# Attention heads in a hand-scheduled decoder trunk: probabilities divided before the transpose, values as the stationary operand, two heads on two column halves, layers written out

## The reference, cut to what matters

```python
# branch A: sparse keys (top-k of an indexer), branch C: causal, branch D: window of 128, with a sink
dots = jnp.einsum('bthd,bsd->bths', qib, ki32)                       # indexer of branch A
iscore = jnp.einsum('bth,bths->bts', wib, jax.nn.relu(dots))
...
s = jnp.where(mask, q @ k.T * scale - slope * dist, NEG)
p = jax.nn.softmax(s, axis=-1)                                       # D: the sink is one more column
o = jnp.einsum('bhts,bshd->bthd', p, v).reshape(B, BLOCK, -1)
...
proj = jnp.einsum('bsnw,nwd->bsnd', ys, w_branch)                    # ys: the four branches' outputs
return jnp.sum(sigmoid(gates) * proj, axis=2) @ w_out
```

## Time and profile before

| | |
|---|---|
| median of 3 runs (lowest, highest) | 2903.86 us (2902.56, 2909.98) |
| profiled execution: its own time | 2905.41 us |
| its span, first to last instruction | 2903.5 us |
| mean granted TensorE clock | 0.992 |
| TensorE matmul / weight load busy | 96% / 79% |
| VectorE / ScalarE / GpSimd busy | 55% / 36% / 6% |
| data moved | 329 MB, 113 GB/s |

### The profile page before, as it was taken

How to read it: one execution, slowest core, us unless ns; L and a number is a source line. 1 busy time by engine, 2 the same in 40 slices (tenths; PEclk the granted TensorE clock), 3 DMA queues, 4 the chain that set the end, 5 groups by cost and what they waited for, 6 DMA issues and landing times.

```text
span 2903.5 us, 40034 instructions
## 1 busy us (share of the span) xinstructions
PE 2793.0 (96%) x13408; PEld 2285.5 (79%) x13408; DVE 1608.6 (55%) x2682; ACT 1038.1 (36%) x1859; POOL 165.5 (6%) x175
## 2 busy tenths in 40 slices
PE   4999999999999999999989999999999999999998
PEld 4888887677778788888878888877777778888887
DVE  6655445667555646633266663466675456565323
ACT  2322234444444433222232222344444453432223
POOL 0111000000000001110011110000000000011100
PEclk9999999999999999999999999999999999999999
DMA  5655422111212224532235544221112223164232
GB/s 229 231 188 181 145 90 77 48 52 59 73 51 95 87 80 174 197 99 94 95 117 202 188 161 143 90 66 52 52 64 68 67 79 102 51 224 174 94 101 95
DMA packets 89157, 329.26 MB, mean 113 GB/s; under 512 B 10018, under 2 KB 10402, under 8 KB 87587
## 3 DMA queue, kind: packets, MB, share of 16 engines
q1 hardware_dynamic: 88994, 327.25, 32.9%
HBM read 325.11 MB, written 2.10 MB: 113 GB/s over the span
## 4 chain that ended last, share of the span: by engine, by line
issue 58%; PE 34%; DVE 2%; DMA 2%; POOL 1%; ACT 1%; DVEq 1%; SPq 0%; ACTq 0%; POOLq 0%
PE bank L447 11%; PE bank L448 11%; PE bank L449 11%; DMA ada_raw<-ada 1%; DMA ada_start<-ada 1%; DVE x L1256 1%; DVEq L1286 1%; PE bank L1455 1%; ACT squares_out L817 1%; POOL wi L571 0%; POOL row_sum L561 0%; POOL rstd_diag L563 0%; DVE ada_start L1327 0%; DVE w_low L431 0%; PE bank L1513 0%
## 5 line engine op out<-in xcount | busy, mean ns | idle before, releaser
L447 PE MATMUL bank<-h_high,w_high 128*128 128x512 f32 (+1 forms) x2528 | 979.1, 387 | 31.1 <-DVE h_low L1277 17.3
L449 PE MATMUL bank<-h_high,w_low 128*128 128x512 f32 (+1 forms) x2528 | 960.7, 380 | 0.0
L448 PE MATMUL bank<-h_low,w_high 128*128 128x512 f32 (+1 forms) x2528 | 960.0, 380 | 0.0
L431 DVE TENSOR_TENSOR w_low<-w_raw,w_high 128x1024 fp32r<-128x1024 f32 x440 | 569.5, 1295 | 606.0 <-ACT w_high L425 603.7
L425 ACT ACTIVATE w_high<-w_raw 128x1024 fp32r<-128x1024 f32 x440 | 461.3, 1050 | 361.7 <-PE bank L456 331.9
L447 PEld LDWEIGHTS bank<-h_high,w_high 128*128 128x128 f32 x2528 | 481.9, 191 | 125.6 <-issue 19.4
L449 PEld LDWEIGHTS bank<-h_high,w_low 128*128 128x128 f32 x2528 | 480.8, 190 | 90.5
L448 PEld LDWEIGHTS bank<-h_low,w_high 128*128 128x128 f32 x2528 | 481.6, 191 | 86.3 <-issue 2.4
L454 PE MATMUL bank<-w_high,ffn_high 128*128 128x512 f32 x704 | 275.6, 391 | 0.0
L456 PE MATMUL bank<-w_low,ffn_high 128*128 128x512 f32 x704 | 273.9, 389 | 0.0
L455 PE MATMUL bank<-w_high,ffn_low 128*128 128x512 f32 x704 | 273.9, 389 | 0.0
(11 more groups left out here) (197 smaller groups left out, 2664.9 us busy)
## 6 DMA issues: line engine op xcount, KB each, us to landing
w_raw<-stream SPq DMA_DIRECT2D x444, 512.0 KB, 3.5
ada_raw<-ada SPq DMA_DIRECT2D x144, 512.0 KB, 3.6
ada_start<-ada SPq DMA_DIRECT2D x8, 1024.0 KB, 16.4
mixer_consts<-mixc SPq DMA_DIRECT2D x2, 1152.0 KB, 5.2
x<-x_in SPq DMA_DIRECT2D x1, 2048.0 KB, 18.1
silu_c<-silu_row SPq DMA_DIRECT2D x4, 512.0 KB, 4.5
out<-x SPq DMA_DIRECT2D x8, 256.0 KB, 2.0
lru_w<-lruw SPq DMA_DIRECT2D x2, 512.0 KB, 3.6
```

What stands on the lines that cost most here:

```text
L431: eng.tensor_tensor(wL[:, slot], raw[:, slot], wH[:, slot].bitcast(F32), ALU.subtract).then_inc(lo_ready[slot].sem, 1)
L447: eng.matmul(o, a, rhs_h, start=first, stop=False)
L448: eng.matmul(o, a, rhs_l, start=False, stop=False)
L449: return eng.matmul(o, b, rhs_h, start=False, stop=last)
```

## The change

What it does:

- Attention: POOL computes the reciprocal of each head's row sum (192 powers with exponent -1), ScalarE multiplies the probabilities by it in place, one step after the exp, and the transposes take the divided probabilities. The lag of the transposes is 3 steps and that of the values 4 (2 and 3 before). There are 4 score slots and 3 slots of transposed probabilities (3 and 2 before).
- The values (64 columns) are the stationary operand and the transposed probabilities (128 columns) the moving one. In every odd step the two heads of a pair are multiplied, alternating over the key blocks, head e into partitions 64e to 64e+63 of bank 7. The result is feature-major, so `y_tok`, its division and its four transposes per block are gone; `y_high` and `y_low` are made from bank 7. The rows of `w_branch` for A and D are permuted on the host to match. A branch has 37 steps.
- D's sink is one more column of the scores (a copy of one column on VectorE for each head), so the sink's own sum and exp are gone.
- Indexer: the dots of a pair of heads are issued together in every even entry, into four banks (4 to 7); entry n waits for the relu of entry n-3.
- The loops over the layers are written out. In the second layer two of three chunks of the modulation product are left out in the second FFN, and so are the loads and splits of the weights of a third layer, and, in the last `closing`, the squares and means of x and their powers.

The core of the diff:

```diff
-TR_LAG, PV_LAG = 2, 3
-END_LAG = HEADS - 1 + PV_LAG
-YT_LAG = END_LAG + 1
+TR_LAG, PV_LAG = 3, 4
+Y_LAG = HEADS - 1 + PV_LAG + 1
...
+def ada_chunks(l, f):
+    return ADA_FFN[f] - (2 if f == 1 and l == DEPTH - 1 else 0)
+
+def ends(l, n):
+    return l == DEPTH - 1 and n == 2
...
+            def reciprocals(l, br, st):
+                g = att_index(br, st)
+                b, h, _, _ = keys(br, st)
+                c = 8 * (b % 2) + h
+                pool.wait_ge(probs_ready.sem, probs_ready.at(l, g + 1))
+                pool.tensor_tensor(recip[:, g % 8:g % 8 + 1], rsum[:, c:c + 1], mone, ALU.pow
+                                   ).then_inc(recip_ready.sem, 1)
...
-            with pool.Fori(0, DEPTH) as l:
+            for l in range(DEPTH):
...
+                    if 1 <= st < STEPS + 1:
+                        g = att_index(br, st - 1)
+                        b, h, k0, nk = keys(br, st - 1)
+                        s.wait_ge(recip_ready.sem, recip_ready.at(l, g + 1))
+                        s.activation(s_sb[:, g % S_SLOTS, 0:P * nk], s_sb[:, g % S_SLOTS, 0:P * nk], ACT.Copy,
+                                     scale=recip[:, g % 8:g % 8 + 1]).then_inc(norm_ready.sem, 1)
...
                     b, h = it[1], it[2]
                     n = HEADS * (b - 1) + h
-                    if n >= 2:
-                        pe.wait_ge(relu_ready.sem, relu_ready.at(l, n - 1))
...
-                    rows = slice(64 * (h % 2), 64 * (h % 2) + 64)
-                    pe.matmul(bank[4 + n % 2][:, 0:P * (b + 1)], iq[rows, h // 2, b * P:(b + 1) * P],
-                              ik[rows, 0:P * (b + 1)], start=True, stop=True).then_inc(dots_ready.sem, 1)
+                    if n >= 4 and n % 2 == 0:
+                        pe.wait_ge(relu_ready.sem, relu_ready.at(l, n - 2))
+                    for i in range(2 if n % 2 == 0 else 0):
+                        rows = slice(64 * i, 64 * i + 64)
+                        pe.matmul(bank[4 + (n + i) % 4][:, 0:P * (b + 1)], iq[rows, h // 2, b * P:(b + 1) * P],
+                                  ik[rows, 0:P * (b + 1)], start=True, stop=True).then_inc(dots_ready.sem, 1)
...
-            if PV_LAG <= st < STEPS + PV_LAG:
+            if PV_LAG <= st < STEPS + PV_LAG and (st - PV_LAG) % 2:
                 g = att_index(br, st - PV_LAG)
+                pair = (st - PV_LAG) % HEADS // 2
                 pe.wait_ge(pt_evicted.sem, pt_evicted.at(l, g + 1))
-                if h == 0 and g > 0:
-                    pe.wait_ge(ytok_ready.sem, ytok_ready.at(l, g // HEADS))
-                for i in range(nk):
...
-                    mm = pe.matmul(bank[7][:, h * HD:(h + 1) * HD], pt_sb[:, g % 2, i * P:(i + 1) * P], vv,
-                                   start=i == 0, stop=i == nk - 1)
+                if pair == 0 and g > 1:
+                    pe.wait_ge(ylo_ready.sem, ylo_ready.at(l, g // HEADS))
+                for i in range(keys(br, st - PV_LAG)[3]):
+                    for e in range(2):
+                        b, h, k0, nk = keys(br, st - PV_LAG - 1 + e)
...
+                        mm = pe.matmul(bank[7][HD * e:HD * e + HD, pair * P:(pair + 1) * P], vv,
+                                       pt_sb[(g - 1 + e) % PT_SLOTS][:, i * P:(i + 1) * P], start=i == 0,
+                                       stop=i == nk - 1)
                 mm.then_inc(pv_done.sem, 1)
-            blk = (st - YT_LAG) // HEADS
-            if st >= YT_LAG and (st - YT_LAG) % HEADS == 0:
...
-                for t in range(4):
-                    mm = pe.transpose(bank[2 + use % 2][:, t * P:(t + 1) * P], y_tok[:, t * P:(t + 1) * P],
-                                      ident[:, :])
-                mm.then_inc(ytr_ready.sem, 1)
```

More of the change, by code:

```diff
@@ L236, in trunk_kernel @@
         S0 = M0 + 57 * K
[L237 to L238 removed]
+        s_sb = at("scores_sb", [P, S_SLOTS, T], F32, S0)
+        pt_sb = [at(f"probs_t{i}", [P, T], F32, w) for i, w in enumerate((S0 + 8 * K, S0 + 10 * K, X0 + 8 * K))]
         relu_sb = at("relu_dots", [P, 2, T], F32, S0 + 6 * K)
[L240 removed]
         bias_sb = at("bias_sb", [P, T], F32, X0 + 10 * K)
@@ L547, in _, with att_index, keys @@
             sp.wait_ge(stored.sem, 16 * 2 * TB)
-            for slot in range(RING):
-                sp.wait_ge(raw_full[slot].sem, raw_full[slot].at(DEPTH, 16))
+        def att_index(br, st):
+            return STEPS * ATT.index(br) + st
+        def keys(br, st):
+            b, h = st // HEADS, HEAD_AT[br][st % HEADS]
+            k0 = max(0, b - 1) if br == "D" else 0
+            return b, h, k0, b + 1 - k0
         @block.gpsimd
@@ L592, in _ @@
                                            ).then_inc(rs_ready.sem, 1)
+                        for br in ATT:
+                            for st in range(STEPS):
+                                reciprocals(l, br, st)
                         closing(l, 1)
@@ L734, in scalar_mixer @@
                     br, st = it[1], it[2]
+                    blk = (st - Y_LAG) // HEADS
+                    if st >= Y_LAG and (st - Y_LAG) % HEADS == 0:
+                        s.wait_ge(pv_done.sem, pv_done.at(l, (att_index(br, 0) + HEADS * (blk + 1)) // 2))
+                        s.activation(yH[Y_OF[br]][:, :, blk * P:(blk + 1) * P],
+                                     bank[7][:, :].rearrange("p (t n) -> p t n", t=4), ACT.Copy
+                                     ).then_inc(yhi_ready.sem, 1)
                     if TR_LAG <= st < STEPS + TR_LAG:
@@ L861, in _ @@
                 squares_x(i // 2, i % 2)
-            with s.Fori(0, DEPTH) as l:
+            for l in range(DEPTH):
                 opening(l, -1, U_FFN[0])
@@ L1156, in vector_attention @@
                 first = nsink[:, h:h + 1] if br == "D" else 3e38
-                v.tensor_tensor_reduce(s_sb[:, g % 3, 0:w], bank[4 + g % 2][:, 0:w], bias, 1.0, first, ALU.add,
+                if br == "D":
+                    v.tensor_copy(s_sb[:, g % S_SLOTS, w:w + 1], nsink[:, h:h + 1])
+                v.tensor_tensor_reduce(s_sb[:, g % S_SLOTS, 0:w], bank[4 + g % 2][:, 0:w], bias, 1.0, first, ALU.add,
                                        ALU.min, nmax[:, c:c + 1]).then_inc(shifted.sem, 1)
-            if br == "C":
-                token_y(v, l, br, st)
-            blk = (st - YT_LAG) // HEADS
-            if st >= YT_LAG and (st - YT_LAG) % HEADS == 0:
+            blk = (st - Y_LAG) // HEADS
+            if st >= Y_LAG and (st - Y_LAG) % HEADS == 0:
                 g = TB * ATT.index(br) + blk
@@ L1211, in vectors @@
                                        ALU.mult, ALU.mult)
-                pre_vector(which)
+                if not ends(l, which):
+                    pre_vector(which)
             def gain_build(l, n):
@@ L1280, in opening @@
                     j = i % KD
-                    if i == 2 and n >= 0:
+                    if i == 2 and (n >= 0 or l > 0):
                         mean_x(l, n, TB - 1)
@@ L1330, in _ @@
             v.scalar_tensor_tensor(vecA[:, :], mod[:, 8 * KD:9 * KD], 1.0, parv[:, 2 * KD:3 * KD], ALU.add, ALU.mult)
-            with v.Fori(0, DEPTH) as l:
+            for l in range(DEPTH):
                 v.drain()
@@ L1691, in _ @@
             pe.wait_ge(consts_in.sem, 16 * 5)
-            with pe.Fori(0, DEPTH) as l:
+            for l in range(DEPTH):
                 for f in range(2):
@@ L1776, in _mixer_units @@
             w = w_branch[branch_at[it[1]]]
+            if it[1] in "AD":
+                w = w[np.concatenate([pairs(0, j) for j in range(4)])]
             out.append(np.concatenate([_tile(w, P * (2 * it[2] + m) + r(P)) for m in range(2)], axis=2))
```

168 lines of the change are left out of this document (62 added, 106 removed).

## The result

The changed kernel takes **2861.47 us** (median of 4, 2861.17 to 2864.06); the kernel before, beside it, 2906.92 (4 runs, 2902.56 to 2910.71). The ratio is 0.9846, 95% interval 0.9828 to 0.9864: 45 us less by the medians, and 44 between the two profiled runs, for which 29 were forecast.

What follows compares the result with a forecast made beforehand. The prediction took TensorE, with a matmul in flight for 96% of the span, as the bound. Its terms summed to -28.8 us from 2905.4, giving 2876.6, less 1.6 to the median: 2875 us; own range 2858 to 2890, whole range 2848 to 2900.

Steps and rivals of the forecast that it cites:

- The indexer: Indexer of both layers: dots in pairs and four banks let TensorE leave 3 to 6.5 us earlier per layer; -10 us.
- Layers written out and the end: Opening between the layers waits less for h_low, -5.7 us; unneeded work behind the last store goes, -1.9 us.
- Attention: Attention branches, both layers: y_tok transposes -10.6, their waits -3.6, values as weights -3, ScalarE and POOL in the chain +6 us.
- Values as weights: Attention's value products: 432 pass pairs at 0.16 us plus 96 groups at 0.13, 81.6 us; -3 us, from -21 to +13.
- estimated gap of 0.053: Value pass pairs: a weight load of half as many columns taken to leave 0.053 us, against 0.10 between score pairs.
- rival B: Attention's values: weight loads run ahead as on the full width, so values take 63 us; 2857 us in all, chance 0.14.
- Waits: TensorE's attention waits: -3.6 us around y_tok and y_low, +6 us at bank 6 behind ScalarE's longer step.
- y_low: Block turns in attention: the next block's first pair waits until VectorE makes y_low from bank 7; 6 us over 18 turns.
- The transposes of y_tok: Attention's block turns: 24 turns of four transposes at 0.44 us each go from TensorE; -10.6 us.
- The clock: TensorE's granted clock over the whole span: the prediction had no term for a change in it.
- Rival A: Attention's values: column halves don't overlap their loads; 2898 us with half-size loads (chance 0.08), 2934 with full-size ones (0.06).
- C: Attention's transposes: ScalarE's longer step holds bank 6, 28 us instead of 6 over 70 steps; 2897 us, chance 0.10.

Runs made afterwards that it cites:

- layers_only: Kernel before with only its layer loops written out and the work behind the last layer left out, attention and indexer unchanged; 2885.23 us, ratio 0.9937.
- no_multiply: Changed kernel without ScalarE's multiplication of the probabilities by the reciprocal, so attention output stays undivided; 2860.48 us, ratio 0.9851 to the kernel before.
- fills_even: Changed kernel with half units of dense work moved: one in every even step, the rest spread over odd steps; 2845.76 us, ratio 0.9815 to the kernel before.
- fills_and_banks: Changed kernel with dense work in every even step plus second banks for transposes and attention output in branch C; 2842.93 us, ratio 0.9802 to the kernel before.

## Why the prediction was right or wrong

By time at full clock, so that the parts add up. They were forecast at 28.8 us and measured at 33.5 by the runs, 36 by the two profiled traces.

- **The indexer, -10: right.** 10.3 and 10.4 in two kernels. TensorE leaves the first one 24.1 us after its first dots.
- **Layers written out and the end, -7.6: measured 10.4.** The boundary opening gave 4.9 in the change (forecast 5.7), the last store 1.8 (forecast 1.9). Not in the sum were the FFN's first products, 2.6 us less of waiting for the activation in layers_only and 4.3 in the change (11.0 to 6.7), and the shorter attention of layers_only.
- **Attention, -11.2: right in the total, wrong in two terms.** Measured 33.5 - 10.4 - 10.4 = 12.7 as what is left of the runs, give or take some 2 us as an estimate from their spread. The total came out by luck, because two terms were off in opposite directions. Added up from TensorE's trace over the three branches and both layers (each instruction from its start to the next start, less the recorded wait, slow stretches at half their length), in us. A matmul behind which TensorE waits stands with its whole duration, so some 0.16 us of each wait are in the rows of the matmuls:

| TensorE's instructions | before | after |
|---|---|---|
| values | 87.1 | 62.0 |
| transposes of the probabilities | 52.4 | 57.9 |
| transposes of y_tok | 10.2 | none |
| scores and dense products | 573.1 | 573.5 |
| waits | 20.2 | 34.7 |
| added by slow stretches | 0 | 3.4 |
| sum | 743.0 | 731.5 |

- *Values as weights, -3, was mis-sized: they gave some 20 us.* Their own rows fell by 25.1, and the transposes in front of them, which hold the entry into the column halves, rose by 5.5. By the median group they take 0.37, 0.59, 0.81 and 1.02 us for one to four key blocks (24, 40, 16 and 16 groups). The step that failed is the estimated gap of 0.053 in a pass pair. There is none; the gap of 0.10 between score pairs doesn't carry over to column halves. The exit and the entry cost a little more than rival B had (0.24 against 0.18 together). So in the values it was B that came true, nearly in full; by itself it would have made the forecast 2857 us.
- *Waits, forecast at 2.4 us more than before, were 14.5 more* (34.7 against 20.2). Of these the third pass of ScalarE is 4 to 5, as no_multiply shows. `neg_max` and L1677's `probs_t`, 4.2 and 2.3, were put at nothing. What was mis-sized most is y_low: 14.7 us, not 6. VectorE, ScalarE and TensorE at such a turn in A, after:

```profile
799.62 0.58 ACT L758 ACTIVATE y_high<-bank 128x512 fp32r<-128x512 f32 x1
...
803.29 0.69 DVE L1063 TENSOR_TENSOR merged<-merged,gated 128x512 f32<-128x512 f32 x1
...
804.61 0.49 PE L1661 MATMUL bank<-ident,scores_sb 128*128 128x128 f32 x3
804.85 0.56 DVE L1152 CUSTOM_DVE_ANT_0 scores_sb<-bank,bias_sb 128x384 f32<-128x384 f32 x1
...
806.25 0.56 DVE L1152 CUSTOM_DVE_ANT_0 scores_sb<-bank,bias_sb 128x384 f32<-128x384 f32 x1
...
806.73 0.69 DVE L1160 TENSOR_TENSOR y_low<-bank,y_high 128x512 fp32r<-128x512 f32 x1
...
807.57 0.88 PE L1677 MATMUL bank<-probs_t,v_tok_a 128*64 128x128 f32 x12 [2.47 <-DVE y_low L1160]
```

ScalarE has made y_high by 800.2 us, but y_low starts 6.5 us later. Ahead of it in VectorE's queue stand four merge passes of a fill (L1060 and L1063, 801.1 to 804.0) and then both score passes of the pair, each with a bias pass ahead of it; TensorE stands for 2.47 us. The prediction had named the score passes ("VectorE's step, which in D and A has two score passes") and still took "up to some 2 us" in few turns; the merge passes it hadn't named. The four longest of these waits (1.8 to 2.8 us, two in each layer, in D and A) all have merge passes and two score passes ahead of y_low. The turn at 662 us in D, with two score passes and no merge, waits 0.99. No run has moved y_low ahead of them, so the order as the cause is read from the trace and not tested.
- **The transposes of y_tok, -10.6: right,** 10.2 by the table. L1683 is gone.
- **The clock, forecast at nothing: 7.4 us.** The sum of the terms missed 15 us (28.8 against the 43.9 between the two profiled runs): 7.4 are the clock, 4.7 the terms above, and 3 that the profiled run before lay above the mean of its runs and the one after a little below. The waits of 1.8 to 2.8 us for y_low took some of the clock back: two of the slow stretches after lie behind them.

So the time fell into the forecast's own range, 2858 to 2890, partly by luck: the values gave what rival B said, the new waits ate most of that, and the clock gave 7 to 8 us that nobody had in the sum.

Rival A is excluded by the timelines. B was right in the price of a pass pair and nearly so in the whole of the values. C didn't come true: bank 6 is waited for 13.3 us, far from 28, and ScalarE's longer step is 2.4 of them, as no_multiply shows. Cover in the even steps takes 7.1 off that wait, as fills_even shows.

What the clock follows is shown in part. A filled pause kept it at 2.4 GHz, four times of four, with an unfilled fifth beside them that didn't. And in the traces of all fourteen kernels together there are 118 slow stretches before TensorE's last product. Each of them begins within a pause of TensorE of more than 1 us or at most 4.0 us behind one, and such moments are under 5% of the time. But a pause doesn't always bring one: of 119 pauses of 2 us or more behind the first 60 us of a run, 47 are followed by none. Why layers_only has full clock behind three of its five openings, with pauses as long as before (2.2 to 2.5 us), is such a case, and isn't settled. Its clocks lie at 0.993 to 0.996 in 6 runs and those of the kernel before at 0.990 to 0.995 in 37, so it is no chance of one run. How much of the 7.4 us comes from fewer pauses and how much from where they fall is not shown.

## What to carry to other kernels

Multiply each run's time by its mean granted clock before you compare: in this kernel, which TensorE bounds, the product is steady to 1 us where the times spread over 14, and parts add up that by medians don't. A pause of TensorE can cost twice, once as a wait and once by the clock behind it. When a change joins two steps into pairs, place the cover work anew: here the same placing of fills gave 19 us with pairs and cost 8 without. The version to keep is fills_and_banks, 2842.9 us, ratio 0.9802 to the kernel before. What no run has tried is y_low ahead of VectorE's merge and score passes; 13.9 us of waits stand there.

## What the runs showed of the hardware

- Loads of a stationary operand on one column half ran ahead of matmuls in flight on the same rows, at 0.11 us per pass of 128 columns, and passes on the two halves overlapped fully (0.11 per pair), for some four passes even where they did not alternate. The Trainium skill ("TensorE: Matmul & The Clock Gate", What overlaps and what doesn't) says that a load overlaps only where the row group differs; the timelines of this case speak against it.
- Going from full-width work to column halves and back costs about 0.09 us on the way in and 0.09 on the way out (least distance L1661 to L1677 0.20 against 0.11, L1677 to a dense product 0.20 against the 0.11 of a pass). The first pair of a group takes another 0.05.
- The granted clock fell to 1.2 GHz for a few microseconds within or behind pauses of 1.1 to 7.8 us in an otherwise busy stream: 118 times in fourteen traces, and never without such a pause, though not behind each one (72 of 119 pauses of 2 us or more). Behind four openings whose pause was filled with 16 idle matmuls it stayed at 2.4 GHz.
